# Two expert tables joined into one gather of 8 KB rows, V products per pair of rows

## The reference

```python
def peer_ffn(xn, w_q, sub_keys, u_tab, v_tab):
    q = (xt @ w_q).astype(jnp.float32).reshape(n_tok, PEER_HEADS, 2, PEER_DHALF)
    scores = jnp.einsum('thcd,ckd->thck', q, sub_keys.astype(jnp.float32))
    top_s, top_i = lax.top_k(scores, PEER_TOPK)
    ...
    sel_s, sel_pos = lax.top_k(cand_s, PEER_TOPK)
    expert_id = jnp.take_along_axis(cand_e, sel_pos, axis=-1).reshape(n_tok, PEER_HEADS * PEER_TOPK)
    gate = jax.nn.softmax(sel_s, axis=-1).reshape(n_tok, PEER_HEADS * PEER_TOPK)

    def block(args):
        xb, eb, gb = args
        act = jax.nn.gelu(jnp.einsum('td,tkd->tk', xb, u_tab[eb]).astype(jnp.float32), approximate=False)
        return jnp.einsum('tk,tkd->td', (gb * act).astype(xb.dtype), v_tab[eb])
```

## Time and profile before

| | us |
|---|---|
| median of 3 runs (lowest, highest) | 3146.85 (3146.2, 3156.86) |
| the profiled execution, span | 3149.5 |
| PE busy | 2364.4 |
| DVE busy | 2255.2 |
| POOL busy | 2127.2 |
| ACT busy | 757.8 |
| gathers' share of the 16 DMA engines | 86.3% |

### The profile page before, as it was taken

The page is one execution under the profiler, slowest core; times in us unless marked ns, Lnnn a source line. Parts: engine busy times, 40 slices in busy tenths (PEclk is TensorE's granted clock), DMA queues, the critical chain, the costliest instruction groups (busy, mean ns, idle before and its releaser), DMA issues.

```text
span 3149.5 us, 33814 instructions
## 1 busy us (share of the span) xinstructions
PE 2364.4 (75%) x11496; PEld 1332.5 (42%) x11496; DVE 2255.2 (72%) x6185; ACT 757.8 (24%) x1295; POOL 2127.2 (68%) x2065
## 2 busy tenths in 40 slices
PE   7888887876776888777867988887766767565655
PEld 6776545432233465554522766654522322111111
DVE  8648888776667788876676677887776667777662
ACT  3522222211111443352101344443211111101000
POOL 0005777777667777777677667777777767777774
PEclk8889888888888899898887899998988888777778
DMA  6219999999999999999999999999999999999996
GB/s 213 68 61 343 405 409 395 409 409 409 409 409 407 402 396 408 393 376 404 409 409 409 404 361 409 398 370 386 406 409 409 409 410 409 409 409 407 408 407 274
DMA packets 329836, 1185.01 MB, mean 376 GB/s; under 512 B 36032, under 2 KB 42176, under 8 KB 329408
## 3 DMA queue, kind: packets, MB, share of 16 engines
q0 software_dynamic: 294912, 1073.87, 86.3%
q1 hardware_dynamic: 34752, 108.98, 9.1%
HBM read 1180.61 MB, written 2.10 MB: 376 GB/s over the span
## 4 chain that ended last, share of the span: by engine, by line
POOL 36%; DMA 21%; PE 20%; issue 15%; DVE 7%; ACT 2%; POOLq 0%; SPq 0%; ACTq 0%; DVEq 0%
POOL arena L614 18%; POOL arena L630 18%; DMA arena<-u_tab,cols 15%; DMA arena<-v_tab,cols 6%; PE ps L676 5%; PE ps L743 4%; PE xps L676 3%; DVE arena L2149 2%; PE xps L1085 1%; PE xps L937 1%; PE ps L756 0%; DVE arena L2250 0%; PE xps L1136 0%; PE xps L923 0%; PE ps L758 0%
## 5 line engine op out<-in xcount | busy, mean ns | idle before, releaser
L614 POOL DMA_INDIRECT arena<-u_tab,cols x1024 | 1061.7, 1037 | 625.5 <-issue 277.9
L743 PE MATMUL ps<-arena,scr 128*32 128x512 f32 x4096 | 1012.6, 745 | 484.2 <-DMA arena<-v_tab,cols 395.9
L630 POOL DMA_INDIRECT arena<-v_tab,cols x1024 | 1061.3, 1036 | 365.1 <-issue 288.2
L2149 DVE CUSTOM_DVE_ANT_0 arena<-arena 128x1024 f32<-128x1024 f32 x624 | 761.9, 1222 | 312.5 <-DMA arena<-u_tab,cols 308.2
L2149 DVE CUSTOM_DVE_ANT_0 arena<-arena,xps 128x1024 f32<-128x1024 f32 x400 | 488.3, 1221 | 341.6 <-DMA arena<-u_tab,cols 337.2
L743 PEld LDWEIGHTS ps<-arena,scr 128*32 128x32 f32 x4096 | 171.8, 122 | 1136.8 <-DMA arena<-v_tab,cols 761.3
L676 PE MATMUL xps<-arena,wring 128*128 128x256 f32 x1600 | 387.6, 393 | 15.3 <-ACT arena L1585 8.2
L676 PEld LDWEIGHTS xps<-arena,wring 128*128 128x128 f32 x1600 | 304.4, 197 | 82.2 <-issue 24.1
L676 PE MATMUL ps<-arena,wring 128*128 128x256 f32 x1184 | 312.9, 428 | 6.0 <-DVE arena L1767 4.2
L676 PEld LDWEIGHTS ps<-arena,wring 128*128 128x128 f32 x1184 | 254.5, 218 | 49.3 <-DVE arena L1767 4.6
L1394 ACT ACTIVATE cols<-cols 128x16 f32<-128x16 f32 x64 | 13.8, 216 | 844.4 <-DVE cols L2149 844.3
(11 more groups left out here) (444 smaller groups left out, 2928.5 us busy)
## 6 DMA issues: line engine op xcount, KB each, us to landing
wring<-wall SPq DMA_DIRECT2D x176, 512.0 KB, 6.8
arena<-u_tab,cols POOLq DMA_INDIRECT x1024, 13.0
arena<-v_tab,cols POOLq DMA_INDIRECT x1024, 13.0
arena<-wall SPq DMA_DIRECT2D x16, 512.0 KB, 9.1
h<-xT SPq DMA_DIRECT2D x2, 1024.0 KB, 11.0
arena<-glu_w SPq DMA_DIRECT2D x2, 1024.0 KB, 12.0
out<-arena SPq DMA_DIRECT2D x4, 512.0 KB, 14.8
arena<-s_b SPq DMA_DIRECT2D x1, 512.0 KB, 9.5
```

The source lines that it names most:

```text
L614: pool.indirect_dma_start(out=uring[:, at % NU, :], out_offset=None, in_=u_tab, in_offset=bass.IndirectOffsetOnAxis(ap=ids[g % 2][:, k:k + ...
L630: pool.indirect_dma_start(out=v_rows(at), out_offset=None, in_=v_tab, in_offset=bass.IndirectOffsetOnAxis(ap=vids[g % 3][:, k:k + 1], axis ...
L743: mm = pe.matmul(ps[4 + half][32 * j:32 * j + 32, :], wdiag[:, n, :], v_rows(at)[:, T * half:T * half + T], start=(g % PH == 0 and b == 0) ...
L2149: dve.tensor_tensor_reduce(uring[:, at % NU, :], uring[:, at % NU, :], x, 1.0, 0.0, ALU.mult, ALU.add, dots[g % 2][:, k:k + 1]).then_inc(s ...
```

## The change

U and V are laid side by side in one table `uv_tab`, 8 KB a row, and one gather fetches both. Since the rows of one gather now serve both the dot and the V product, both have the same layout: a gather holds 2 experts for each of 64 tokens. So 16 gathers of 1 MB stand where 32 of 512 KB stood in a round.

- The ring has 8 such buffers (`NS`), 15 from round 46 on. A buffer is free only once its V products are done.
- The ids and gates of half the experts have to reach the other half of the partitions: PE does it with a matmul by `swap` (`swap_ids`, `swap_gates`), DVE copies them (`ids_across`, `gates_across`).
- The token rows are needed twice, once for each set of 64 tokens: `xrep` has two buffers, both in use, and `to_rows` runs in four steps at the border between tiles instead of two steps earlier. The copies to PSUM are gone.
- Gelu (`gelus`), the blocks (`weights`, now `place` times gelu times gate, 64 columns each) and the V products (`values`, 4 products of 64 output rows x 512 columns) are done for each pair of rows, 8 times a round: the blocks behind the next dot, the products one slot later. Spreading and `spread_w` are gone.
- `y_rows`, `finish` and `tile_done` of a tile stand 16 slots earlier.

```diff
-NU = 6
-NV = 10
+NS = 8
+NS_LONG = 15
+PAIRS = 4
...
+def rows_at(t, i):
+    return TOPK * PH * t + (-1, -0.5, 0.5, 1)[i]
...
+            def gather(g, k):
                 at = g * TOPK + k
                 if k == 0:
                     pool.wait_ge(s["ids_ready"], g + 1)
...
+                if SLOT_BEFORE[at] is not None:
+                    pool.wait_ge(s["v_free"], SLOT_BEFORE[at] // 2 * 2 + 2)
                 pool.indirect_dma_start(
+                    out=whole_row(at), out_offset=None, in_=uv_tab,
...
             def values(g, b):
-                if b == 0:
-                    pe.wait_ge(s["w_ready"], g + 1)
...
+                pe.wait_ge(s["w_ready"], 8 * g + b + 1)
...
                 for half in range(2):
-                    for j in range(4):
...
-                        mm = pe.matmul(ps[4 + half][32 * j:32 * j + 32, :], wdiag[:, n, :],
+                    for j in range(2):
+                        mm = pe.matmul(ps[4 + half][64 * j:64 * j + 64, :], wdiag[:, b % PAIRS, j, :],
...
             def to_rows(t, i):
                 act.wait_ge(s["side_mm"], SIDE_MM["x", t, i])
...
+                if t:
+                    act.wait_ge(s["dot_done"], PH * TOPK * t - 1 + i // 2)
...
+            def gelus(g, b):
+                act.wait_ge(s["dot_done"], g * TOPK + 2 * b + 2)
...
+            def weights(g, b):
+                dve.wait_ge(s["gelu_ready"], 8 * g + b + 1)
+                if b == 0:
+                    dve.wait_ge(s["gate_found"], 2 * g + 2)
+                if 8 * g + b >= PAIRS:
+                    dve.wait_ge(s["v_free"], 2 * (8 * g + b - PAIRS) + 2)
+                for n in (2 * b, 2 * b + 1):
+                    m = stt(wdiag[:, b % PAIRS, n % 2, :], place, gelu[g % 2][:, n:n + 1],
+                            gate[g % 2][:, n:n + 1].to_broadcast([P, 64]), ALU.mult, ALU.mult)
+                m.then_inc(s["w_ready"], 1)
...
             for r in range(ROUNDS + 1):
                 for k in range(TOPK):
                     if r < ROUNDS:
                         dot(r, k)
+                    if r and k == 0:
+                        weights(r - 1, 7)
+                    if r < ROUNDS and k >= 2 and k % 2 == 0:
+                        weights(r, k // 2 - 1)
```

More of the change, by code:

```diff
@@ L1263, in _ @@
             first_rows(1, 1, range(2, DC))
-            to_rows(0, 0)
-            to_rows(0, 1)
+            swap_ids(0)
+            for i in range(4):
+                to_rows(0, i)
             first_sum(1)
+            swap_gates(0)
             first_query(1)
@@ L1293, in _ @@
                         scores(*queries[now - 4.5])
-                    if k in (10.5, 11.5) and r in rows:
-                        to_rows(rows[r], int(k > 11))
-                    if k == (13 if r == 0 else 10.5) and r + 1 < ROUNDS:
-                        spread_ids(r + 1)
+                    if now in rows:
+                        to_rows(*rows[now])
+                    if k == 8.5 and r + 1 < ROUNDS:
+                        swap_ids(r + 1)
+                    if k == 12.5 and r + 1 < ROUNDS:
+                        swap_gates(r + 1)
                     for part in paced:
                         part.upto(TOPK * r + k)
-            values(ROUNDS - 1, 3)
-            for i in range(3):
-                finish(2 * TT - 1, i)
         @block.scalar
@@ L1707, in _ @@
             queries = {query_at(gi, q): (gi, q) for gi in range(4) for q in range(PH) if gi or q > 1}
-            rows = {ROWS_ROUND[t]: t for t in ROWS_ROUND}
+            rows = {rows_at(t, i): (t, i) for t in range(1, 2 * TT) for i in range(4)}
             for r in range(ROUNDS + 1):
-                done = r // PH - 1 if r % PH == 1 and r > PH else None
+                done = r // PH - 1 if r % PH == 0 and r else None
                 for x in range(2 * TOPK):
@@ L1733, in _ @@
                         part.upto(TOPK * r + k)
-            y_rows(2 * TT - 1)
-            for i in range(3):
-                finish(2 * TT - 1, i)
         @block.vector
@@ L2135, in value_ids, with ids_across @@
+            def ids_across(g):
                 dve.wait_ge(s["ids_mm"], g + 1)
[L2136 removed]
+                for hf in range(2):
+                    m = ts(other_half(ids[g % 2], hf), ps[6][64 * hf:64 * hf + 64, 0:8], float(g // HEADS * E), None,
+                           ALU.add)
+                m.then_inc(s["ids_ready"], 1)
             def dot(g, k):
                 at = g * TOPK + k
[L2141 to L2142 removed]
```

268 lines of the change are left out of this document (111 added, 157 removed).

## The result

The changed kernel takes 3208.27 us (median of 4 runs, 3203.91 to 3210.23) against 3146.52 us of the kernel before, run beside it: 1.0192 times as long, with an interval of 1.0168 to 1.0215. It is slower by 62 us; 3201 was forecast. The profiled execution has a span of 3202.0 us, against 3149.5 before.

The account below looks back on a forecast made before the run. Transfers were taken to bound most rounds, PE some of the mixers' rounds. 3149.5 - 51 - 20.5 + 3 + 51 + 9.9 + 52 + 10 = 3203.9, 3201 us as median, 1.7% slower; range 3085 to 3340.

Parts of the forecast that it names:

- V products: PE in the mixers' rounds: two products fit side by side instead of four, 15.4 us a round for 7.70; +51 us.
- lockstep on ACT: Rounds with mixer work: a Gelu late behind ACT's queue delays blocks and products, 2 us in each of 26 rounds; +52 us.
- Transfers: Gathers in 51 transfer-bound rounds: half the packets at 8 ns each saves 1.0 us a round; -51 us.
- V-only end: After the last dots: 16 V gathers no longer stand alone, -20.5 us; one dot, Gelu, blocks and products follow, +3.
- 95.5%: PE's busy share in round 34 (56.8 of 59.5 us), taken as PE's limit where it bounds.
- Round 0: First round, which had no V products before: PE gets 15.4 us more, 63.2 us for 53.3; +9.9 us.
- The waits that I had named as signs: Mixers' rounds: DVE's L2145 waiting for ACT's L1376, and PE's L737 for DVE's L2145, tens of us each.
- Spare in the chain: From a pair's landing to the next gather into its buffer: 4 to 6 us to spare beside the other six buffers' transfers.
- Borders: Between tiles: token rows can't be turned ahead, so the second dot comes late; 2 us at each of 5 borders, +10 us.
- Before the first dot: Start of the kernel: the prediction's sum had no term for it.
- The closed chain: Dot, next dot, Gelu, blocks, products before a buffer pair is free, 7.3 to 9 us: no cost of its own.
- the ring smooths it: Rival for the whole kernel: the spare evens out full and light rounds, ACT is never late; 3088 us, chance 0.27.

Follow-up runs that it names:

- run 3: The changed kernel with the blocks made from the dots instead of their Gelu, so ACT is waited for only a round later: 3199.69 us, 1.0173.
- Run 4: The changed kernel with each 8 KB gather made as two gathers of 4 KB rows into the same buffer: 3357.14 us, 1.0657.
- run 1: The kernel before with every V product issued twice: 3193.84 us, 1.014.
- run 2: The changed kernel with V products of 256 columns in place of 512, but for a tile's first product: 3159.3 us, 1.0042.
- Run 5: The changed kernel without turning the token rows of every half after the first: 3183.41 us, 1.0118.
- run 8: The changed kernel with its token-row transposes placed otherwise at the start and the later borders, all work kept: 3192.27 us, 1.0152.
- Run 6: The changed kernel with 256-column V products, blocks made from the dots without Gelu, and no token-row turning after the first half: 3122.34 us, 0.992.

## Why the prediction held, point by point

The time came out 7 us over the forecast and the sign was right, and the V products, which carry it, were sized right in their sum. That the time came so near is luck: the step that failed is the lockstep on ACT, put at 52 us where run 3 shows 8, 44 us too high. What I had at nothing or too low made up for it: the first dot 9.5, the turning up to 11, a remainder of some 22 whose cause is open, together 42. Without the 44 the sum would have been 3157 us, hardly a change.

- **Transfers, -51.** The 420 GB/s came as worked out, but rounds 46 to 63 gained 0.7 us each for 1.0, and round 59 by itself took 40.9, which alone would have denied the term. Single rounds scatter: rounds 57 to 63 took 40.0 each for 41.2, rounds 49 to 55 42.3 for 42.9. Where the other 0.3 us stays isn't shown. The 0.45 us a round worked out from the Trainium skill's 3 cycles a packet would have been too little. Run 4, made to price the packets, ran into POOL's issuing instead. In the mixers' rounds the gain can't be told apart.
- **V-only end, -20.5, and +3 behind it.** -18.5 together for -17.5.
- **V products, +51.** 15.50 us of PE in round 38 for 15.4, up to 17.6 where the windows hold part of another round's. Rounds 33, 34, 36 and 38 took 43.6, 72.3, 60.1 and 50.7 us, 226.7 in all for 203.3, where +29 was forecast and +23.4 came. Runs 1 and 2 put the term at 47 to 49 by the medians. This was the step that carried the sign, and two runs from opposite sides confirm it. Its split by rounds was wrong: of the 29 us in these four rounds the products alone account for 12 (run 1) to 16 (run 2), since PE's other work moved from round 33 to 34, and more lies in rounds 17 to 26, 12 to 18 us for the 11 forecast. Nor is 95.5% PE's limit, as I had it: PE was busy 98.8% of round 34 and 99.6% of round 38.
- **Round 0, +9.9.** +9.5 came, for another reason. I had PE's capacity in it; run 2 halved the products, and the round stayed (63.8). It moves with the ring (67.4 with 7 buffers, 73.3 with 6): POOL's longest wait, 34.4 us, lies here, for products that stand behind the second half's projections in PE's order. The rows that I summed couldn't show that, since they gave busy time and not order.
- **Lockstep on ACT, +52.** This is the term that failed. Run 3 gives 8 us, and not in rounds 33 to 38. I had counted a late Gelu as PE's time; PE waits for the blocks 545.5 us with ACT and 541.1 without it. The waits that I had named as signs were there, and hardly a cost: cut by stretch, first rounds 33 to 38, then 46 to 62, they lie for the most part where PE has room.

```profile
PE ps L737 <- DVE scr L2145: 14.6, 9, 3.2
```

```profile
PE ps L737 <- DVE scr L2145: 232.0, 110, 4.1
```

- **Spare in the chain, 4 to 6 us.** That was too much for part of the rounds: one buffer less, 2.5 us of transfers, already costs 61 us in all, and two cost 274.
- **Borders, +10.** Run 5 bounds it at 21 us. Rounds 24 and 40 have more than that, but from `finish`, moved a round ahead onto full rounds, which isn't in my sum; rounds 41 to 45 gave it back.
- **Before the first dot, 0.** +9.5 came. I had said of `to_rows` only that it stands at the borders, and hadn't followed the four steps of the first half, which the diff puts ahead of the second half's squares: 4 x (1.98 + 0.6) us in PE's and ACT's order. Moving three of them behind gave 5.8 us back in run 8.
- **The closed chain, 0.** I had it at nothing for itself, as the spare covered it. Run 6 leaves some 22 us in rounds 1 to 45, with neither ACT nor long products nor turning in them. Shown is the size of the remainder, reckoned as if every one of these rounds could gain 0.7 us, though PE bounds some of them; it isn't shown that the chain is its cause. It lies in rounds 1 to 5, 24 and 33 to 38, where PE has most to do, and 5.6 us of it in round 24, to which `finish` was moved.

Of the rivals, "the ring smooths it" was wrong for its own reason: PE's peaks come through at 47 us. It was right that ACT is hardly ever late in a way that counts. The row that would have told stands in the earlier trace rows: with PE busy 56.8 of 59.5 us in round 34, a late Gelu can be covered by PE's own backlog, and run 3 bears that out.

## What to carry to other kernels

When a layout changes how many products fit side by side on PE, price that first, in the rounds where PE is already full; here it was 47 us, against 0.7 us a round from larger packets. A new wait in the profile is priced by asking who would be late without it, not by its length. And follow every step that a new layout adds at the start and at borders through the order of its engines: the cheapest find here (the transposes moved, 16 us) was in it.

## What the hardware showed

Two things weren't expected. An indirect gather's issue on POOL that begins inside a dot on DVE with both inputs in SBUF (1.22 us, 128 x 1024 floats) lasts until 0.81 us after that operation's end (1.52 us in the mean for 268 of them), beside one with an input in PSUM it takes its 0.94 us; with 32 gathers a round and all dots of this kind, POOL was the bound (45.4 us a round for 40.0). And a kernel with 32 gathers of 4 KB rows a round took 3395 us on one chip and 3147 on others, while one with 16 gathers of 8 KB rows took 3204 there and 3192 elsewhere; the cause is open.
